# Attention scores whose low-part products contract 64 rows, two maps in two row groups of the array

## What is computed

```python
def diff_attend(q, k, v, lam):
    s = jnp.einsum('bhmqd,bhmkd->bhmqk', q, k).astype(jnp.float32) * (QK_DIM ** -0.5)
    p = jax.nn.softmax(s, axis=-1)
    p = p[:, :, 0] - lam * p[:, :, 1]
    return jnp.einsum('bhqk,bhkd->bhqd', p.astype(v.dtype), v)
```

## Time and profile before

| | before |
|---|---|
| median of 3 runs | 1965.02 us |
| the profiled execution | 1965.6 us, of which the span of its core is 1964.3 us |
| mean granted TensorE clock | 0.995 |
| PE busy | 1910.6 us, 97% of the span |
| DVE busy | 1346.9 us, 69% |
| ACT busy | 834.8 us, 42% |
| POOL busy | 131.7 us, 7% |

### The profile page before, as it was taken

How to read it: one execution, slowest core, us unless ns; L and a number is a source line. 1 busy time by engine, 2 the same in 40 slices (tenths; PEclk the granted TensorE clock), 3 DMA queues, 4 the chain that set the end, 5 groups by cost and what they waited for, 6 DMA issues and landing times.

```text
span 1964.3 us, 30435 instructions
## 1 busy us (share of the span) xinstructions
PE 1910.6 (97%) x12296; PEld 1599.4 (81%) x12296; DVE 1346.9 (69%) x2031; ACT 834.8 (42%) x1512; POOL 131.7 (7%) x158
## 2 busy tenths in 40 slices
PE   6999999999999999999999999999999999999997
PEld 3888888877888887888888888888888888888886
DVE  6788887768878788765776346657965677634554
ACT  5356665135667472333542222336233463212221
POOL 0011201001111101000000000000101000000000
PEclk9999999999999999999999999999999999999999
DMA  8322222333323546523354335434642234433332
GB/s 317 116 71 76 76 76 75 106 113 97 97 65 108 171 126 226 151 87 85 92 177 144 104 117 172 134 103 138 219 139 76 86 110 149 121 104 91 92 108 75
DMA packets 298171, 235.17 MB, mean 120 GB/s; under 512 B 6832, under 2 KB 273584, under 8 KB 297008
## 3 DMA queue, kind: packets, MB, share of 16 engines
q1 hardware_dynamic: 278880, 163.49, 28.1%
q0 software_dynamic: 18432, 67.12, 10.2%
q10 hardware_dynamic: 720, 2.62, 0.4%
HBM read 231.10 MB, written 2.10 MB: 119 GB/s over the span
## 4 chain that ended last, share of the span: by engine, by line
PE 81%; DVE 11%; issue 4%; ACT 3%; DMA 1%; POOL 0%; DVEq 0%; SPq 0%; ACTq 0%; POOLq 0%
PE ps L657 63%; PE ps L630 4%; PE ps L676 3%; PE ps L1602 2%; DVE w_lo_second L606 1%; PE ps L1581 1%; PE ps L1582 1%; DVE mod_products_in L1021 1%; PE ps L1613 1%; DVE w_lo_first L606 1%; PE ps L2783 1%; ACT a_p L1915 1%; DVE attention_stats L2107 1%; DVE pool_pad L2026 1%; PE ps L2400 1%
## 5 line engine op out<-in xcount | busy, mean ns | idle before, releaser
L657 PE MATMUL ps<-h_second_hi,w_hi_second 128*128 128x512 f32 x992 | 390.7, 394 | 0.0
L657 PE MATMUL ps<-h_second_lo,w_hi_second 128*128 128x512 f32 x992 | 386.5, 390 | 0.0
L606 DVE TENSOR_TENSOR w_lo_second<-w_raw_second,w_hi_second 128x1024 fp32r<-128x1024 f32 x168 | 204.9, 1220 | 85.3 <-ACT w_hi_second L598 85.2
L657 PE MATMUL ps<-h_second_hi,w_lo_second 128*128 128x512 f32 x992 | 246.1, 390 | 1.5 <-DVE w_lo_second L606 1.5
L657 PEld LDWEIGHTS ps<-h_second_hi,w_lo_second 128*128 128x128 f32 x992 | 186.0, 188 | 42.1 <-DVE w_lo_second L606 3.2
L657 PEld LDWEIGHTS ps<-h_second_hi,w_hi_second 128*128 128x128 f32 x992 | 186.4, 188 | 37.6 <-DVE h_second_lo L916 0.2
L657 PEld LDWEIGHTS ps<-h_second_lo,w_hi_second 128*128 128x128 f32 x992 | 186.5, 188 | 37.0
L598 ACT ACTIVATE w_hi_second<-w_raw_second 128x1024 fp32r<-128x1024 f32 x168 | 175.7, 1049 | 79.5 <-PE ps L676 42.7
L657 PE MATMUL ps<-h_hi,w_hi_first 128*128 128x512 f32 (+1 forms) x592 | 203.3, 357 | 0.9 <-DVE proj L1997 0.8
L657 PE MATMUL ps<-h_lo,w_hi_first 128*128 128x512 f32 (+1 forms) x592 | 199.8, 351 | 0.0
L3162 ACT ACTIVATE conv<-ps,cols 128x512 f32<-128x512 f32 x44 | 34.3, 780 | 249.2 <-PE ps L657 248.5
(11 more groups left out here) (355 smaller groups left out, 3610.1 us busy)
## 6 DMA issues: line engine op xcount, KB each, us to landing
w_raw_second<-in_w_in SPq DMA_DIRECT2D x64, 512.0 KB, 4.5
w_raw_first<-in_w_in SPq DMA_DIRECT2D x48, 512.0 KB, 3.9
mod_w_mixer<-in_ada_w_turned POOLq DMA_DIRECT2D x48, 512.0 KB, 4.0
w_raw_second<-in_w_gate SPq DMA_DIRECT2D x44, 512.0 KB, 4.0
w_raw_second<-in_w_val SPq DMA_DIRECT2D x44, 512.0 KB, 4.5
w_raw_down<-in_w_down SPq DMA_DIRECT2D x32, 704.0 KB, 4.7
mod_w_ffn<-in_ada_w_turned POOLq DMA_DIRECT2D x32, 512.0 KB, 3.7
mod_w_in<-in_w_mod_turned POOLq DMA_DIRECT2D x27, 512.0 KB, 3.6
```

The lines of the kernel that those rows point to most:

```text
L606: k.nc.vector.tensor_tensor(lo, raw, hi.bitcast(F32), ALU.subtract).then_inc(k.sem.weight_split, 1)
L657: last = tensor.matmul(k.ps[:, bank, 0:count], w[:, q * P:(q + 1) * P], rows[q][:, first:first + count], start=(n == 1), stop=(n == 3 * t.k))
```

## The change

The products with the keys' low parts take only the 64 rows of their map: rows 0 to 63 of `a_q[0]` and `proj_r` for map 0, rows 64 to 127 for map 1. `a_qz`, `pad_scalar` and `clear_padding` go, with the semaphores `a_padded` and `a_cleared`. In a unit, the 4 (or 2) products over 128 rows come first, then the low products: for a full unit 6 pieces of 256 columns each, with map 1 and map 0 in turn, for a context unit 2. Only the first low product of a full unit raises a new semaphore `low_scored`, and TensorE itself waits for it ahead of the sixth, since the first and the sixth are of different maps and both write bank 3. Which product opens and which closes a bank's accumulation is now written in the tables.

```diff
-    tensor.wait_ge(n.a_padded, 2 * at + 2)
-
-    for m, bank, column, b, w in SCORE_PIECES[j >= TX // P]:
-        out, keys = k.ps[:, bank, column:column + w], slice(first + b, first + b + w)
-        tensor.matmul(out, k.a_q[m][:, cut], k.a_khi[m][:, keys], start=True, stop=False)
-        last = tensor.matmul(out, k.a_qz[:, at % 2, m, :], k.proj_r[:, 4 + 3 * h, keys], start=False, stop=True)
+
+    for m, bank, column, b, w, opens in SCORE_PIECES[j >= TX // P]:
+        tensor.matmul(k.ps[:, bank, column:column + w], k.a_q[m][:, cut], k.a_khi[m][:, first + b:first + b + w],
+                      start=opens, stop=False)
+    for i, (m, bank, column, b, closes) in enumerate(LOW_PIECES[j >= TX // P]):
+        rows = HALVES[m]
+        if i == 5:
+            tensor.wait_ge(n.low_scored, QUERIES[1] * (HEADS * l + h) + j + 1)
+        last = tensor.matmul(k.ps[:, bank, column:column + TC], k.a_q[m][rows, cut],
+                             k.proj_r[rows, 4 + 3 * h, first + b:first + b + TC], start=False, stop=closes)
+        if i == 0 and j < TX // P:
+            last.then_inc(n.low_scored, 1)
     last.then_inc(n.scored, 1)

+SCORE_PIECES = (((0, 2, 0, 0, TX, True), (1, 4, 0, TC, TX, True), (0, 3, 0, TX, TC, True), (1, 3, TC, 0, TC, False)),
+                ((0, 2, 0, 0, TC, True), (1, 3, TC, 0, TC, True)))
+LOW_PIECES = (((1, 3, TC, 0, False), (0, 2, 0, 0, False), (1, 4, 0, TC, False), (0, 2, TC, TC, True),
+               (1, 4, TC, TX, True), (0, 3, 0, TX, True)),
+              ((0, 2, 0, 0, True), (1, 3, TC, 0, True)))
-def pad_scalar(k, l, h, j):
-    ...
-    for m in (0, 1):
-        scalar.activation(k.a_qz[HALVES[m], at % 2, m, :], k.a_q[m][HALVES[m], j * P:(j + 1) * P], ACT.Copy).then_inc(
-            n.a_padded, 1)
-def clear_padding(k, l):
-    ...
```

More of the change, by code:

```diff
@@ L194 @@
     gate_curved
-    a_prepared_a a_prepared_v a_prepared_g a_cleared a_padded scored biased exped p_combined p_turned p_moved headed head_stored
+    a_prepared_a a_prepared_v a_prepared_g low_scored scored biased exped p_combined p_turned p_moved headed head_stored
     head_varied head_inverted head_scaled head_turned head_gated
@@ L317, in place_first @@
         self.conditions = self.place("conditions", [P, 2, D])
-        self.a_qz = self.place("a_query_padded", [P, 2, 2, P], F32R, at=self.top)
         self.lamv = self.place("lamv", [P, 2, 4, QK], at=self.top)
@@ L1576, in score_tensor @@
         tensor.wait_ge(n.exped, 2 * at)
-    tensor.wait_ge(n.a_padded, 2 * at + 2)
-    for m, bank, column, b, w in SCORE_PIECES[j >= TX // P]:
-        out, keys = k.ps[:, bank, column:column + w], slice(first + b, first + b + w)
-        tensor.matmul(out, k.a_q[m][:, cut], k.a_khi[m][:, keys], start=True, stop=False)
-        last = tensor.matmul(out, k.a_qz[:, at % 2, m, :], k.proj_r[:, 4 + 3 * h, keys], start=False, stop=True)
-    last.then_inc(n.scored, 1)
-SCORE_PIECES = (((0, 2, 0, 0, TX), (1, 4, 0, TC, TX), (0, 3, 0, TX, TC), (1, 3, TC, 0, TC)),
-                ((0, 2, 0, 0, TC), (1, 3, TC, 0, TC)))
+    for m, bank, column, b, w, opens in SCORE_PIECES[j >= TX // P]:
[9 more added lines that the diff above has]
+            last.then_inc(n.low_scored, 1)
+    last.then_inc(n.scored, 1)
+SCORE_PIECES = (((0, 2, 0, 0, TX, True), (1, 4, 0, TC, TX, True), (0, 3, 0, TX, TC, True), (1, 3, TC, 0, TC, False)),
[3 more added lines that the diff above has]
+              ((0, 2, 0, 0, True), (1, 3, TC, 0, True)))
 def attention_tensor(k, l, s):
@@ L1904, in attention_scalar @@
                           k.banks(5, count).rearrange("p (c n) -> p c n", n=P), ACT.Copy).then_inc(n.p_moved, 1)
-    for h, j in scored_at(l, s + 2):
-        pad_scalar(k, l, h, j)
     for h, j in scored_at(l, s - 1):
@@ L1963, in first_vector @@
             maxima_vector(k, l, h, j)
-        if s == 25:
-            clear_padding(k, l)
         if s in (13, 17):
```

## The result

The changed kernel takes 1969.07 us as the median of 13 runs (1967.46 to 1971.62), the kernel before 1965.25 us in 13 runs beside it (1963.28 to 1967.49): a ratio of 1.0018, with a 95% interval of 1.0011 to 1.0026. It is slower by 3.8 us, between 2.2 and 5.1. Unchanged copies of it, timed twice more, gave 1.0016 (1.0008 to 1.0025) and 1.0020 (1.0011 to 1.0029). The forecast was slower by 8.

The account below looks back on a forecast made before the run. TensorE was taken as the bound, busy 97% of the span. From 1965.6 us, its added 10.2 us at 0.90 gave +9.2 and ScalarE's relief -1: 1973.8, less 0.6 for the median, rounded to 1973.0; range 1958 to 1978.

Parts of the forecast that it names:

- the 10.2 us: Attention scores: TensorE's forecast added work, 32 x 0.25 us for full units plus 8 x 0.28 for context units.
- the sum: TensorE per unit: full 0.95 us in place of 0.70, +0.25; context 0.52 in place of 0.236, +0.28.
- the relief: ScalarE loses 80 padding copies (24.6 us), VectorE 4 clears: -1 us taken at the end, range 0 to -2.5.
- That TensorE's time is what counts: In both attentions TensorE's time counts nearly in full, ScalarE's hardly at all; TensorE busy 97% of the span.
- The switch: Leaving and re-entering full-array form around low products: 0.08 in, 0.11 and 0.11 for loads, 0.10 out, 0.40 us an excursion.
- the overlap of loads and of streams: Low products of the two row halves load and stream side by side, so three pairs stream in 0.35 us.
- the wait: TensorE waits for its first low product ahead of the sixth, 0.43 us; low stage 0.66 us in place of 0.46.
- rival 1: Low products: row halves overlap and switching is free, but the wait remains; faster, 1958.8 us, chance 0.25.
- rival 2: Low products: the halves' loads or products go one after the other, switch paid; slower still, 1976.9 us, chance 0.13.
- rival 3: Low products: row halves neither switched to nor overlapped; the same, 1964.3 us, chance 0.12.
- the share of 0.90: Scores in both attentions: 0.90 of each microsecond added or saved on TensorE reaches the end, from 43.5 / 48.6 us.
- at most one pair of copies, 0.6 us, a wait: TensorE's attention waits for ScalarE, six places: each can shrink by at most 0.6 us, all by less than 4 us.

Follow-up runs that it names:

- filler: Kernel before with two more 256-column products at the start of each of 40 units' scores: 1976.05 us, ratio 1.0057.
- filler_early: Kernel before with three idle 256-column products ahead of the scores of 30 of the 40 units: 1976.73 us, ratio 1.0060.
- again_before: Kernel before, unchanged, timed and profiled once more: 1965.68 us, ratio 1.0000.
- again_after: Changed kernel, unchanged, timed and profiled once more: 1968.73 us.
- again_after2: Changed kernel, unchanged, timed again as base beside the run with the padding's work kept: 1969.30 us.
- pads_kept: Changed kernel with the old padding's 80 copies, 4 clears and their waits still done, result unused: 1971.09 us, ratio 1.0028.
- filler_late: Kernel before with three idle 256-column products right behind the scores of 30 of the 40 units: 1974.81 us, ratio 1.0051.
- padded_keys: Kernel before with the keys' low parts padded in place of the queries, whole output computed: 1966.95 us, ratio 1.0010.
- no_pad: Kernel before without the padding's 80 ScalarE copies and 4 VectorE clears, TensorE's work the same: 1964.10 us, ratio 0.9992.
- four_excursions: Changed kernel with each low product right behind its high one, four excursions a full unit, two a context unit: 2010.15 us (2 runs).
- unpaired: Changed kernel with low products issued as three of map 1, then three of map 0: 1969.49 us, ratio 1.0022.

## Why the forecast was right in its sign and too large

The starts of the same products in nine profiles, in us, show where the 10.2 us went. "First narrow" is the first 32-column product of the second block (L2678 in the kernel before), "last group" the first of the 16 full-array products that end the same work on the same operands (L2754). The fillers' profiles have a fall of the clock at 289 (late), two at 418 and 452 (first filler), one at 453 (late) and one at 451 (early); the profiled execution of filler_early was its fastest, 4.3 us under its median.

| | unit 1 | unit 24 | unit 25 | unit 40 | first narrow | last group | span |
|---|---|---|---|---|---|---|---|
| before | 119.75 | 317.81 | 483.32 | 630.33 | 750.05 | 809.41 | 1964.3 |
| again_before | 120.14 | 320.71 | 483.96 | 630.99 | 751.07 | 810.36 | 1968.6 |
| changed | 118.85 | 321.80 | 485.46 | 634.00 | 753.89 | 812.10 | 1966.9 |
| again_after | 119.20 | 322.24 | 486.04 | 634.51 | 754.47 | 812.82 | 1967.4 |
| again_after2 | 119.13 | 320.95 | 486.26 | 634.76 | 754.64 | 812.77 | 1967.4 |
| pads_kept | 118.01 | 321.04 | 484.61 | 634.67 | 754.59 | 814.11 | 1969.0 |
| filler | 118.48 | 320.41 | 487.00 | 636.87 | 759.48 | 819.20 | 1974.7 |
| filler_late | 119.81 | 323.38 | 488.43 | 638.51 | 760.34 | 818.50 | 1974.1 |
| filler_early | 118.78 | 321.59 | 486.44 | 636.91 | 758.16 | 816.29 | 1970.8 |

**Layer 0**, units 1 to 24: 198.06 us before and 201.82 in again_after2, the two without a fall of the clock in that stretch: +3.8, where the sum has 16 x 0.25 + 7 x 0.28 = 6.0. The missing 2.2 us are waits of TensorE that shrank. In the kernel before:

```profile
185.82 0.47 PE L1581 MATMUL ps<-a_khi,a_q 128*128 128x512 f32 x1 [1.94 <-issue]
230.75 0.50 PE L1581 MATMUL ps<-a_khi,a_q 128*128 128x512 f32 x1 [0.56 <-ACT a_p L1915]
238.90 0.63 PE L1549 MATMUL ps<-squares,proj 128*128 128x128 f32 x4 [1.00 <-DVE inverse_roots L2048]
284.37 0.50 PE L1581 MATMUL ps<-a_khi,a_q 128*128 128x512 f32 x1 [2.31 <-ACT a_p L1915]
291.24 0.47 PE L1581 MATMUL ps<-a_khi,a_q 128*128 128x512 f32 x1 [0.33 <-issue]
314.62 0.63 PE L1655 MATMUL ps<-squares,proj 128*128 128x128 f32 x4 [1.05 <-DVE proj L2159]
```

and in the changed kernel:

```profile
186.45 0.93 PE L1578 MATMUL ps<-a_khi,a_q 128*128 128x512 f32 x4 [1.49 <-ACT a_p L1896]
240.41 0.63 PE L1548 MATMUL ps<-squares,proj 128*128 128x128 f32 x4 [0.70 <-DVE inverse_roots L2027]
286.94 0.96 PE L1578 MATMUL ps<-a_khi,a_q 128*128 128x512 f32 x4 [2.06 <-ACT a_p L1896]
318.61 0.63 PE L1663 MATMUL ps<-squares,proj 128*128 128x128 f32 x4 [0.76 <-DVE proj L2138]
```

7.19 us in six waits became 5.01 in four (4.99 in again_after2, whose stretch is the one without a fall). Two more waits, of 0.34 and 0.80 us, are the same in both. The profile puts four of the six down to VectorE or ScalarE and two to nothing ("issue"), but in padded_keys the same two, 1.99 and 0.38 us there, end with the exponentials. TensorE's lateness is made up in part at each of them: what it waits for comes later than before as well, but by less. The exponential that ends the first comes 1.5 us later than before, counted from each trace's first unit, and the wait is 0.45 us shorter for it.

**Layer 1**, units 25 to 40: 147.01 and 147.03 us before, 148.54, 148.47 and 148.50 in the changed kernel, 150.06 with the padding's work kept. The sum has 15 x 0.25 = 3.75: with the padding's work 3.05 of it arrive, and the relief takes off 1.55, so 1.5 are left.

**The second block.** From the first narrow product to the last group it is 59.36 and 59.29 us before, and 58.21, 58.35 and 58.13 in the changed kernel, whose instructions there are the same: 1.1 us given back in each of its profiles. It is a single wait of TensorE. The kernel before has this one (0.95 us in its second profile), and the changed kernel has none there:

```profile
782.33 0.24 PE L2745 MATMUL ps<-g_query,g_key 128*32 128x16 f32 x4 [1.13 <-issue]
```

With the padding's work kept the stretch is 59.52, and a wait stands 11 us earlier in it:

```profile
771.39 0.79 PE L2755 MATMUL ps<-g_query,g_key 128*32 128x16 f32 x72 [1.17 <-DVE g_decay L3049]
```

The stretch takes one of two lengths in the other runs too: 59.72 in the first filler, but 58.16 and 58.13 in its late and early twins, 58.20 in no_pad and 58.22 in padded_keys. So neither the padding nor the row halves decide it, and what does stays open: the profile names no releaser for the wait of the kernel before.

Together: 3.8 + 1.5 + 0.25 for the last unit + 0.28 for the 24th - 1.1 = 4.7 us, inside the interval of 2.2 to 5.1. The rest, to 3.8, is less than one fall of the clock. The 1.1 us has no cause that is known, so a part of the small result is luck.

Step by step. That TensorE's time is what counts held. The switch (0.09 in for 0.08, 0.11 for each bare load, 0.09 out for 0.10), the overlap of loads and of streams, and the wait (0.44 for 0.43) were each right within 0.02 us, so rivals 1, 2 and 3 are out by the timeline, and rival 1 also by four_excursions. The Trainium skill's rule that changing the mode drains the engine ("TensorEngine Tiling (Array Packing)", Key Properties) agrees with the 0.09 us either way, and what it says of packing, that products in different row groups run side by side ("TensorE: Matmul & The Clock Gate", Part 3), agrees with the two starts at 119.72. The two bare loads, 0.11 us each, cost more here than the two drains.

Two terms were mis-sized. The first is the share of 0.90 that I took from the chain. It says how much of the scores' time lies on the longest path as it was. It is measured on TensorE's own stretches, and it can't say that where the path comes in from VectorE or ScalarE, TensorE had up to 2.3 us of slack just ahead of the unit, in which a part of the time added since the last such point vanishes. From unit 1 to unit 40 the share that arrives is much the same whatever was added: 6.9 of 9.7 us with the padding's work kept (3.05, and for layer 0 the 3.8 of the stretch without a fall), which is 0.71, and 6.7 of 9.0, 7.5 of 10.3 and 8.2 of 10.6 for the three fillers, 0.73 to 0.77 (the late one less 1.1 for its fall). So 0.90 was too high by about 0.2.

The rest of the difference lies behind the attention, in the 120 us from unit 40 to the first narrow product, where hardly anything was added. They are 119.7 and 120.1 us before, 119.9 to 120.0 in the changed kernel, and 122.6, 121.8 and 121.3 with the fillers, because at the second block's norm TensorE then waits for VectorE. The first filler:

```profile
712.85 0.43 PE L612 MATMUL ps<-squares,summed_squares 128*32 128x1 f32 x32 [0.85 <-DVE summed_squares L825]
716.13 0.65 PE L794 MATMUL ps<-squares,inverse_roots 128*128 128x128 f32 x4 [1.24 <-DVE inverse_roots L1106]
```

The same two waits are 1.9 and 1.7 us in its late and early twins, and at most 0.5 in the kernel before and the changed kernel. Why the fillers meet them is open. By the medians 10.2 us cost 5.1 (pads_kept against the kernel before), with an interval of 3.7 to 7.3; the stretches give 7.4. For the fillers the medians are 9.7 to 11.6, from 9.4 and 10.6 us.

The second is ScalarE's relief: -1 was taken and 1.4 and 1.8 measured (1.6 and 1.7 in layer 1 by the traces), within the bounds given. The rule "at most one pair of copies, 0.6 us, a wait" held (0.6, 0.6 and 0.5), but one of the three was a wait for VectorE, which shrank with ScalarE's copies all the same, and I hadn't counted those.

The range of 1958 to 1978 holds rivals of both signs, so it says little that 1969.07 lies in it. What the prediction got right is TensorE's sum, term by term; what it got wrong is how much of it reaches the end.

## What to carry to other kernels

Leaving the full-array form has a fixed price, here some 0.4 us an excursion, half of it weight loads that can't run ahead; pairing has to save more than that in one excursion, and six products of 256 columns can save 0.35 at most (three pairs of 0.118 in place of 0.70). An engine that waits for its own product puts that product's whole latency (0.44 us) into its stream: here 0.20 us a unit, and 3.7 us in the kernel. An experiment that reorders products has to be read in the timeline before its time is: unpaired changed the order of issue, and the pairs ran as before. To turn time added on the busiest engine into time at the end, list that engine's waits along the way and ask of each whether it will swallow the delay; the chain's share alone doesn't say it. Here it was 0.90, and 0.71 to 0.77 of four additions arrived at the end of the attention; then the next norm added up to 2.6 us to some of them and nothing to others. Read such a share stretch by stretch, since the median of the whole kernel mixes them.

## What was not expected of the hardware

The 64-row halves load their weights fully side by side: two loads of 128 columns start 3 ns apart and the pair streams 0.11 us later, as one would. The halves also don't keep the order of issue between them: with three products of one map issued ahead of three of the other (unpaired), the two maps' first products start 10 ns apart, and the loads with them. TensorE's granted clock fell to its lower level, 1.2 GHz (0.50 in 414 to 418 us of the first profile of before), for some microseconds after waits of up to 3 us, at other places in other executions of one kernel, and each fall cost 1.1 to 2.3 us, as much as half of the effect that was to be measured. And the same stretch of 59.3 us in the second block took 1.1 us less in kernels that differ only in the first, by one wait of TensorE that is there or not.
